# The down projection as seven products of halves, with GpSimd making the sums of its weights once

## The chip, the cores and the metric

One core of one Trainium2 chip runs the whole layer in a single launch. The metric is device microseconds (us) of one execution. The kernel before takes 3103.75 us (median of three runs, 3103.4 to 3106.19). Five engines work side by side: TensorE (PE, with its weight loads as PEld), VectorE (DVE), ScalarE (ACT), GpSimd (POOL) and SyncE (SP). They wait for one another through semaphores. DMAs are issued from SP's and POOL's queues.

## The reference, cut to what matters

Two sequences of 1024 tokens with 1024 channels go through one encoder layer. The token mixer (neighbourhood attention beside a two-way scan) is untouched. What follows it is the channel mixer, whose last product is the one that changes:

```
h = rms_norm(x, norm_ffn_pre)                                  # (tokens 1024, 1024)
gate = depthwise_conv(h @ w_gate, ffn_conv_w, ffn_conv_b)      # (1024, 2816)
f = (gelu(gate) * (h @ w_up)) @ w_down                         # w_down: (2816, 1024)
return x + rms_norm(f, norm_ffn_post)
```

All arrays are float32 in DRAM.

## The kernel before, in words

The two sequences run one after the other (`s` = 0, 1). Activations are kept with channels on the partitions, 128 at a time. Every product in float32 is made of three matmuls in a rounded format: an operand is split into a high part and the rest, and high times high, high times rest and rest times high are added up in PSUM (`product`, lines 574 to 579). Weights come in *units* of 128 x 512 (four blocks of 128 x 128): SP loads a unit into one of four `raw` slots, ACT writes its high part (`whi`, three slots, line 1130), DVE subtracts to get the rest (`wlo`, line 1636), PE uses it for 12 matmuls of 512 columns and sets `weights_used`, which frees the slot. `JOBS` lists the order of the products; `UNITS_TO` and `RELEASE` derive the units and the waits from it. SP, ACT and DVE follow this one list, each ahead of PE by as much as the slots allow.

The gate and up projections (job kind `seven`) already use seven products of halves for each of 20 of the 22 blocks of 128 of the inner width 2816: seven units a block, with DVE forming the sums of weights (lines 2098 to 2112). The result of block p is f(p), 128 x 1024 tokens, made by `f_product`. The first 12 blocks of f don't fit and are sent to DRAM by POOL (line 2482), and brought back at the end of this stage (`f_back`, lines 2486 to 2497): three transfers of 1 MB with the first halves of the tokens, then one of 3 MB with the second halves.

The down projection (job kind `down`, lines 1074 to 1092) is then 16 jobs: 2 halves of the tokens times 8 blocks of 128 output channels. A job adds up 22 blocks of f, so 22 x 3 matmuls, in one PSUM bank. f is split too: ACT writes the high part (`f_first`, line 1522), DVE the rest in place (`f_rest`, line 2125), all 22 blocks of a half at the start of that half, in the order `DOWN_CHUNKS`. After each job ACT copies the bank out (line 1569).

While the second half runs, the first four of the eight token tiles of the result are turned back by PE (`tail_tile`, line 640), normalised (`tail_stats`, `tail_out`) and saved, with `x1_ring` holding three tiles of the residual that POOL fetches (line 2324). The other four tiles come after the stage: for sequence 0 inside the start of sequence 1, for sequence 1 at the very end. In sequence 0 SP also fetches the eight tiles of the next sequence's input (`load_x`, line 526), all at once when the second half has begun, before the next weights in its queue.

## Time and profile before

| | |
|---|---|
| median of three runs | 3103.75 us |
| the profiled execution | 3104.28 us, of which the span of its records is 3102.5 us |
| granted TensorE clock, mean | 0.98 of full speed |
| PE busy | 2941.6 us (95%) |
| DVE, ACT, POOL busy | 60%, 41%, 16% |
| down projection, sequence 0 | 1282.15 to 1547.08 us |
| down projection, sequence 1 | 2821.52 to 3076.84 us |

A row of the profile names a line of the kernel, an engine, what is written and from what. PE's matmuls overlap: a row of 0.40 us stands every 0.23 us, so their pace is read from the starts. The clock is given as a share of 2.4 GHz; 0.50 would be 1.2 GHz throughout a stretch. The idle time before a row is followed by what ended it.

### The profile page before, as it was taken

Reading aid. Unit: us, or ns where it says so; the run is one execution under the profiler, and the core shown is the slowest. Engines: PE = TensorE matmul, PEld = TensorE weight load, DVE = VectorE, ACT = ScalarE, POOL = GpSimd, SP = SyncE. Lnnn points to the kernel's source line nnn. Section 1 sums busy time; section 2 is a strip of 40 time slices with the busy share of each in tenths; the row PEclk is TensorE's granted clock in tenths of the full one; section 3 lists DMA queues with packets and bytes.
Section 4 is the critical chain, followed back from the end, with each engine's and each line's share of the span. In section 5 each row is a group of like instructions: output and inputs, shape, how many; then the busy total and the mean of one; then the engine's idle time right before and its main releaser. Section 6 shows DMA issues by size and latency. Waiting matters only on the chain.

```text
span 3102.5 us, 37254 instructions
## 1 busy us (share of the span) xinstructions
PE 2941.6 (95%) x13432; PEld 2336.7 (75%) x13432; DVE 1855.1 (60%) x2915; ACT 1281.0 (41%) x2526; POOL 496.5 (16%) x730
## 2 busy tenths in 40 slices
PE   7999999899899999999999999989998999999997
PEld 5778787568678888787777787766786788887775
DVE  3657745765477777724336577457655777776342
ACT  4225555365543333424333255544655333334332
POOL 4522223540000000000000322236300000000000
PEclk9999999999999999999999999999998999999998
DMA  7441233024322211435321422331242222115342
GB/s 215 128 141 56 71 116 128 26 71 125 109 74 79 79 61 55 159 96 182 111 81 58 130 63 72 111 119 32 78 143 85 69 81 82 62 55 168 90 157 88
DMA packets 136055, 302.89 MB, mean 98 GB/s; under 512 B 16881, under 2 KB 21649, under 8 KB 135872
## 3 DMA queue, kind: packets, MB, share of 16 engines
q1 hardware_dynamic: 104848, 193.61, 20.4%
q0 software_dynamic: 31024, 106.90, 10.7%
q8 instruction: 108, 1.77, 0.2%
q14 instruction: 75, 0.61, 0.1%
HBM read 246.14 MB, written 56.26 MB: 97 GB/s over the span
## 4 chain that ended last, share of the span: by engine, by line
PE 77%; DVE 10%; issue 4%; POOL 4%; ACT 4%; DMA 1%; SPq 0%; DVEq 0%; ACTq 0%; POOLq 0%
PE G L577 11%; PE G L578 11%; PE G L579 11%; PE A L1029 4%; PE A L1028 4%; PE A L1027 4%; PE G L1027 4%; PE G L1029 4%; PE G L1028 4%; PE G L607 2%; PE G L608 2%; PE G L609 2%; PE A L748 2%; DVE arena L1783 2%; POOL arena L2411 2%
## 5 line engine op out<-in xcount | busy, mean ns | idle before, releaser
L1636 DVE TENSOR_TENSOR wlo<-raw,whi 128x512 fp32r<-128x512 f32 x620 | 418.5, 681 | 747.4 <-ACT whi L1130 746.7
L577 PE MATMUL G<-arena_rounded,whi 128*128 128x512 f32 x1792 | 730.8, 408 | 20.8 <-DVE wlo L1636 11.7
L579 PE MATMUL G<-arena_rounded,wlo 128*128 128x512 f32 x1792 | 712.0, 397 | 0.0
L578 PE MATMUL G<-arena_rounded,whi 128*128 128x512 f32 x1728 | 687.2, 398 | 0.0
L1130 ACT CAST whi<-raw 128x512 fp32r<-128x512 f32 x620 | 371.3, 608 | 571.8 <-PE G L579 451.4
L577 PEld LDWEIGHTS G<-arena_rounded,whi 128*128 128x128 f32 x1792 | 339.7, 190 | 109.2 <-issue 17.6
L579 PEld LDWEIGHTS G<-arena_rounded,wlo 128*128 128x128 f32 x1792 | 339.1, 189 | 82.1
L578 PEld LDWEIGHTS G<-arena_rounded,whi 128*128 128x128 f32 x1728 | 327.4, 189 | 76.2
L1027 PE MATMUL G<-arena_rounded,whi 128*128 128x512 f32 x560 | 221.7, 396 | 1.3 <-DVE small L2174 1.3
L1029 PE MATMUL G<-arena_rounded,wlo 128*128 128x512 f32 x560 | 221.5, 396 | 0.0
L1027 PE MATMUL A<-arena_rounded,whi 128*128 128x512 f32 x560 | 221.5, 396 | 0.0
L1028 PE MATMUL A<-arena_rounded,whi 128*128 128x512 f32 x560 | 221.5, 396 | 0.0
L1029 PE MATMUL A<-arena_rounded,wlo 128*128 128x512 f32 x560 | 221.5, 396 | 0.0
L1028 PE MATMUL G<-arena_rounded,whi 128*128 128x512 f32 x560 | 221.5, 395 | 0.0
L1130 ACT CAST whi<-small 128x512 fp32r<-128x512 f32 x160 | 99.1, 621 | 220.3 <-DVE small L2106 86.9
L607 PE MATMUL G<-whi,arena_rounded 128*128 128x512 f32 x320 | 138.5, 433 | 8.9 <-ACT small L1262 4.7
L1293 ACT ACTIVATE small<-small,nmx 128x192 f32<-128x192 f32 (+3 forms) x128 | 66.3, 518 | 188.1 <-DVE nmx L1840 188.1
L608 PE MATMUL G<-wlo,arena_rounded 128*128 128x512 f32 x320 | 126.4, 395 | 0.0
L609 PE MATMUL G<-whi,arena_rounded 128*128 128x512 f32 x320 | 126.3, 395 | 0.0
L1027 PEld LDWEIGHTS G<-arena_rounded,whi 128*128 128x128 f32 x560 | 105.2, 188 | 27.5 <-DVE small L2174 2.2
L1636 DVE TENSOR_TENSOR wlo<-small,whi 128x512 fp32r<-128x512 f32 x160 | 110.0, 687 | 24.8 <-ACT whi L1130 20.8
L1028 PEld LDWEIGHTS A<-arena_rounded,whi 128*128 128x128 f32 x560 | 105.2, 188 | 25.4
(312 smaller groups left out, 4788.2 us busy)
## 6 DMA issues: line engine op xcount, KB each, us to landing
raw<-w_gu_tiles SPq DMA_DIRECT2D x184, 256.0 KB, 3.1
raw<-w_down_tiles SPq DMA_DIRECT2D x160, 256.0 KB, 2.7
raw<-w_tok_tiles SPq DMA_DIRECT2D x96, 256.0 KB, 2.7
raw<-w_out_tiles SPq DMA_DIRECT2D x96, 256.0 KB, 2.7
raw<-w_in_tiles SPq DMA_DIRECT2D x92, 256.0 KB, 2.7
f_by_chunk<-small POOLq DMA_DIRECT2D x24, 512.0 KB, 4.5
arena<-x SPq DMA_DIRECT2D x16, 512.0 KB, 8.6
gate_by_token<-small POOLq DMA_DIRECT2D x16, 512.0 KB, 4.1
```

The lines of the kernel that those rows point to most:

```text
L577: nc.tensor.matmul(out, whi[:, u % SPLIT_SLOTS, w], hi, start=first, stop=False)
L578: nc.tensor.matmul(out, whi[:, u % SPLIT_SLOTS, w], lo, start=False, stop=False)
L579: return nc.tensor.matmul(out, wlo[:, u % SPLIT_SLOTS, w], hi, start=False, stop=last)
L607: nc.tensor.matmul(bank(i), h_hi(k, half)[:, cs], w_hi, start=k == 0, stop=False)
L608: nc.tensor.matmul(bank(i), h_hi(k, half)[:, cs], w_lo, start=False, stop=False)
L609: m = nc.tensor.matmul(bank(i), h_lo(k, half)[:, cs], w_hi, start=False, stop=k == KD - 1)
L1027: nc.tensor.matmul(bank, w_hi, hi(kk), start=kk == 0 and not onto, stop=False, skip_group_check=True)
L1028: nc.tensor.matmul(bank, w_hi, lo(kk), start=False, stop=False, skip_group_check=True)
L1029: m = nc.tensor.matmul(bank, w_lo, hi(kk), start=False, stop=kk == UC - 1, skip_group_check=True)
L1130: nc.scalar.copy(whi[:, u % SPLIT_SLOTS, w], weights_of(u)).then_inc(S["hi_split"], 1)
L1293: nc.scalar.activation(p_, p_, ACT.Exp, bias=nmx[:, st % 2:st % 2 + 1], accum_out=rsum[:, st % 2:st % 2 + 1]).then_inc(S["p_exp"], 1)
L1636: tt(wlo[:, u % SPLIT_SLOTS, w], weights_of(u), whi[:, u % SPLIT_SLOTS, w].bitcast(F), ALU.subtract).then_inc(S["lo_split"], 1)
```

## The change

The down projection is done by seven products of halves. The inner width of 2816 is cut into two sets of 11 blocks (`K1`, `K2`), the 1024 tokens and the 1024 output channels into halves of 512. Instead of eight products of half by half there are seven (`PRODUCTS`), on the halves themselves (`a11`, `a22`, `a12`) or on sums of them (`s1` to `s4`). Each runs over 11 units. A unit is now one block of 128 of the inner width by 512 output channels, for one set of four PSUM banks: 4 banks x 3 matmuls. Partial results stay in the banks from one product to the next where they are needed again (`onto`), and are copied out by ACT (`copy_down`, products 0 to 3) or added by DVE (`add_down`, products 4 to 6).

f goes through a ring of four pairs of a high part and a rest (`ring`), one pair a unit. DVE also forms the sums of f: `t1_made` in product 0, `t_made` two units ahead in products 1 to 3. The sums of the weights are made once, by GpSimd, while sequence 0 is in the gate and up stage: for each of 11 pairs of blocks two loads, four element-wise operations of 128 x 512 and two stores to DRAM (`sums_of_down`). The input of the next sequence is fetched tile by tile between weight loads (`X_LOADED`), into halves of blocks of f that are done with; the tail tiles use other banks (`tail_pair`) and stand in products 5 and 6 (`TAILS_AT`). Some semaphores for single steps of ACT are merged into one (`after`).

```diff
-JOBS += [("down", j, (h,)) for h in range(2) for j in range(KD)]
+JOBS += [("down", o, (0, 1)) for o in range(7)]
-CHUNKS = {..., "down": FK}
+CHUNKS = {..., "down": FK // 2 * UC}
...
+K1 = tuple(range(12, 20)) + (4, 5, 6)
+K2 = (7, 0, 1, 2, 3, 8, 9, 10, 11, 20, 21)
+PRODUCTS = ("a11", "s2", "s3", "a22", "a12", "s1", "s4")
+RING = (0, 1, 8, 9)
+X_LOADED = (37, 41, 57, 60, 45, 63, 66, 69)
+TAILS_AT = ((5, 3), (5, 5), (6, 0), (6, 2))
...
 # SP
-                for job in range(J_OUT + EARLY, J_DOWN + KD + 1):
+                for job in range(J_OUT + EARLY, J_DOWN + 1):
                     load(job)
-                if s + 1 < SEQS:
-                    sp.wait_ge(S["weights_used"], nth("weights_used", UNITS_TO[J_DOWN + KD]))
-                    load_x(s + 1)
-                for job in range(J_DOWN + KD + 1, len(JOBS)):
-                    load(job)
+                sp.wait_ge(S["sw_saved"], 32 * HALF_K)
+                for n in range(HALF_K, 7 * HALF_K):
+                    o, i = divmod(n, HALF_K)
+                    if n in X_LOADED and s + 1 < SEQS:
+                        at_x = X_LOADED.index(n)
+                        sp.wait_ge(S["weights_used"], nth("weights_used", UNITS_TO[J_DOWN + (3 if at_x in (0, 1, 4) else 5)]))
+                        load_x(s + 1, (at_x,))
+                    load(J_DOWN + o, slice(i, i + 1))
...
 # PE, in place of the loop over 16 jobs
+                    out, w = down_banks(o)[:, b, :], slice(b * P, (b + 1) * P)
+                    nc.tensor.matmul(out, w_hi, ring(n, 0), start=i == 0 and not onto, stop=False, skip_group_check=True)
+                    nc.tensor.matmul(out, w_hi, ring(n, 1), start=False, stop=False, skip_group_check=True)
+                    return nc.tensor.matmul(out, w_lo, ring(n, 0), start=False, stop=i == HALF_K - 1, skip_group_check=True)
...
+                for o in range(7):
+                    for i in range(HALF_K - 2):
+                        parts_ready_for(o, i)
+                        for b in range(4):
+                            if i == 0:
+                                if 1 <= o <= 3:
+                                    pe.wait_ge(S["d_copied"], nth("d_copied", 4 * (o - 1) + b + 1))
...
+                                elif o == 6:
+                                    pe.wait_ge(S["d_added"], nth("d_added", 4 + b + 1))
+                            m = part_of_down(o, i, b)
+                        m.then_inc(S["weights_used"], 1)
...
+                    for i in range(HALF_K - 2, HALF_K):
+                        parts_ready_for(o, i)
+                    for b in range(4):
+                        m = part_of_down(o, HALF_K - 2, b)
+                        if b == 3:
+                            m.then_inc(S["weights_used"], 1)
+                        m = part_of_down(o, HALF_K - 1, b)
+                        m.then_inc(S["d_done" if b < 3 else "weights_used"], 1)
...
 # ACT
+                def f_first(n):
+                    o, i = divmod(n, HALF_K)
+                    act.wait_ge(S["weights_used"], nth("weights_used", UNITS_TO[J_DOWN] + (n - 3 if n >= 4 else -6)))
...
+                    elif o < 4:
+                        act.wait_ge(S["ft_made"], nth("ft_made", n + 1))
+                    nc.scalar.copy(ring(n, 0), of_f(n)).then_inc(S["fhi_done"], 1)
...
+                for n in range(7 * HALF_K):
+                    o, i = divmod(n, HALF_K)
+                    if n >= 4:
+                        f_first(n)
+                    if i == 1 and 1 <= o <= 4:
+                        for b in range(3):
+                            copy_down(o - 1, b)
+                    split_to(UNITS_TO[J_DOWN] + n + 1)
+                    if i == 1 and 1 <= o <= 4:
+                        copy_down(o - 1, 3)
...
 # DVE
+                def t1_made(i):
+                    second_half_of(K1[i])
+                    dve.wait_ge(S["flo_done"], nth("flo_done", i + 1))
+                    tt(f_at(K1[i], 0), f_at(K1[i], 1), f_at(K1[i], 0), ALU.subtract).then_inc(S["ft_made"], 1)
...
+                    if s == 0 and p == F_KEPT + 4:
+                        dve.wait_ge(S["sw_saved"], 32 * HALF_K)
...
+                for n in range(7 * HALF_K):
+                    o, i = divmod(n, HALF_K)
+                    if n >= 4:
+                        f_rest(n)
+                    if i == 1 and o >= 5:
+                        for b in range(3):
+                            add_down(o - 1, b)
+                    split_to(UNITS_TO[J_DOWN] + n + 1)
+                    if i == 1 and o >= 5:
+                        add_down(o - 1, 3)
+                    if o == 0:
+                        t1_made(i)
+                    if HALF_K <= n + 2 < 4 * HALF_K:
+                        t_made(*divmod(n + 2, HALF_K))
...
 # POOL
+                def sums_of_down(i):
...
+                    pool.dma_start(first, w_down[K1[i]]).then_inc(S["sw_in"], 16)
+                    pool.dma_start(second, w_down[K2[i]]).then_inc(S["sw_in"], 16)
+                    pool.wait_ge(S["sw_in"], 32 * (i + 1))
+                    for to, a, b, op in ((a22, a21, a22, ALU.add), (a21, a11, a21, ALU.subtract),
+                                                        (a11, a22, a11, ALU.subtract), (a12, a12, a11, ALU.subtract)):
+                        nc.gpsimd.tensor_tensor(to, a, b, op).then_inc(S["pool_step"], 1)
+                        pool.wait_ge(S["pool_step"], step())
+                    pool.dma_start(sw_dram[i, 0], first).then_inc(S["sw_saved"], 16)
+                    pool.dma_start(sw_dram[i, 1], second).then_inc(S["sw_saved"], 16)
...
                 for p in range(F_KEPT):
                     pool.wait_ge(S["f_ready"], nth("f_ready", p + 1))
                     settled()
                     pool.dma_start(f_dram[p], f_home(p)).then_inc(S[f"f_moved{p % 2}"], 16)
+                    if s == 0 and p:
+                        sums_of_down(p - 1)
...
-                pool.wait_ge(S["weights_used"], nth("weights_used", UNITS_TO[J_DOWN + KD]))
+                pool.wait_ge(S["weights_used"], nth("weights_used", UNITS_TO[J_DOWN + 5]))
```

Three places show how the order moves. First DVE's queue from the end of the gate and up stage into the down projection. Before, `L2125` is `f_rest`, `L1636` the rest of a weight unit, `L2117` to `L2079` the last block's gate and convolution, `L2090` its product:

```order
L1636 TENSOR_TENSOR wlo<-raw,whi 128x512 x2
L2125 TENSOR_TENSOR arena_rounded<-arena,arena_rounded 128x512 x2
L2117 TENSOR_TENSOR small<-G,small 128x512
L2075 TENSOR_SCALAR small<-small,prm 128x1024
L2077 SCALAR_TENSOR_TENSOR small<-small,prm 128x1024
L2079 SCALAR_TENSOR_TENSOR small<-small,prm 128x1024
L1636 TENSOR_TENSOR wlo<-raw,whi 128x512
L2125 TENSOR_TENSOR arena_rounded<-arena,arena_rounded 128x512 x4
L1636 TENSOR_TENSOR wlo<-raw,whi 128x512
L2125 TENSOR_TENSOR arena_rounded<-arena,arena_rounded 128x512 x4
```

The same place now; `L1719` is the rest of a weight unit, `L2207` is `f_rest`, `L2224` is `t1_made`, and `L2200`, `L2158`, `L2160`, `L2162` are the gate and the convolution:

```order
L1719 TENSOR_TENSOR wlo<-raw,whi 128x512 x2
L2200 TENSOR_TENSOR small<-G,small 128x512
L2224 TENSOR_TENSOR arena<-arena 128x512 x2
L2158 TENSOR_SCALAR small<-small,prm 128x1024
L1719 TENSOR_TENSOR wlo<-raw,whi 128x512
L2224 TENSOR_TENSOR arena<-arena 128x512
L2160 SCALAR_TENSOR_TENSOR small<-small,prm 128x1024
L1719 TENSOR_TENSOR wlo<-raw,whi 128x512
L2224 TENSOR_TENSOR arena<-arena 128x512
L2162 SCALAR_TENSOR_TENSOR small<-small,prm 128x1024
L2207 TENSOR_TENSOR arena_rounded<-arena,arena_rounded 128x512
L1719 TENSOR_TENSOR wlo<-raw,whi 128x512
```

The splits of f, in fours before, stand singly beside each weight unit now, with a sum of f behind them, and the convolution is spread over three units.

Second, POOL's queue in the gate and up stage of sequence 0. Before, it has nothing there but the transfers of f to DRAM and back:

```order
L2478 MEMSET small 128x1
L2482 DMA f_by_chunk<-small 128x1024 x12
L2489 DMA arena<-f_by_chunk 128x4x512 x3
L2489 DMA arena<-f_by_chunk 128x12x512
```

Now, from the second block of f on, the sums of one pair of weight blocks follow each transfer (`L2623` are the four operations):

```order
L2633 DMA f_by_chunk<-small 128x1024 x2
L2618 DMA arena<-w_down_rows 128x1024
L2619 DMA arena<-w_down_rows 128x1024
L2623 TENSOR_TENSOR arena<-arena 128x512 x4
L2625 DMA sums_of_down<-arena 128x1024
L2626 DMA sums_of_down<-arena 128x1024
L2633 DMA f_by_chunk<-small 128x1024
```

Eleven such groups stand in the queue, and each later transfer of f is queued behind one.

Third, SP's queue in the down projection of sequence 0, where the next input is fetched. Before:

```order
L520 DMA raw<-w_down_tiles 128x512 x5
L520 DMA raw<-w_down_tiles 128x256
L526 DMA arena<-x 128x2x512 x8
L520 DMA raw<-w_down_tiles 128x512 x5
```

Now, from unit 33 on (`L567` are weights, `L573` the tiles of the input):

```order
L567 DMA raw<-w_down_rows 128x512 x4
L573 DMA arena<-x 128x2x512
L567 DMA raw<-w_down_rows 128x512 x4
L573 DMA arena<-x 128x2x512
L567 DMA raw<-w_down_rows 128x512 x4
L573 DMA arena<-x 128x2x512
L567 DMA raw<-w_down_rows 128x512 x10
L567 DMA raw<-sums_of_down 128x512 x2
L573 DMA arena<-x 128x2x512
L567 DMA raw<-sums_of_down 128x512 x3
```

Eight transfers in a row have become single ones, three before unit 46 and five from unit 57 on.

## Rows read from the trace of the kernel before

**Rows 1.** The page, part 1: busy us, share, instructions of each engine.
```profile
PE 2941.6 (95%) x13432; PEld 2336.7 (75%) x13432; DVE 1855.1 (60%) x2915; ACT 1281.0 (41%) x2526; POOL 496.5 (16%) x730
```

**Rows 2.** Stretches: length, busy us by engine, granted clock, DMA share, GB/s.
```profile
1282.15:1547.08 264.93, 255.90 (x1089) 204.24 (x1088) 102.71 (x158) 97.44 (x177) 8.63 (x12) 0.98 0.45 141
2821.52:3076.84 255.32, 251.55 (x1089) 200.93 (x1087) 97.04 (x148) 88.31 (x159) 8.24 (x12) 1.00 0.41 125
1410.00:1420.00 10.00, 10.00 (x43) 7.57 (x42) 8.12 (x14) 2.56 (x5) 0.15 (x1) 1.00 1.01 357
1430.00:1440.00 10.00, 10.00 (x32) 7.91 (x33) 5.03 (x7) 4.57 (x8) 0.68 (x1) 0.70 0.39 124
1490.00:1500.00 10.00, 10.00 (x38) 7.96 (x37) 1.71 (x3) 1.27 (x3) 0.70 (x1) 0.83 0.56 169
890.00:1260.00 370.00, 370.00 (x1587) 298.11 (x1586) 278.27 (x379) 117.44 (x191) 5.86 (x11) 1.00 0.21 70
```

**Rows 3.** Timeline of PE, last unit before the down projection: start, length, engine, line.
```profile
1276.79 0.39 PE L1028 MATMUL G<-arena_rounded,whi 128*128 128x512 f32 x1
...
1281.92 0.40 PE L1029 MATMUL G<-arena_rounded,wlo 128*128 128x512 f32 x1
```

**Rows 4.** PE groups, the first two stretches: busy, mean | idle, releasers.
```profile
L577 PE MATMUL G<-arena_rounded,whi 128*128 128x512 f32 x352 | 141.9, 403 | 9.0 <-DVE wlo L1636 5.9 <-issue 1.9 <-DVE arena_rounded L2125 1.3
...
L577 PE MATMUL G<-arena_rounded,whi 128*128 128x512 f32 x352 | 140.1, 398 | 3.8 <-issue 1.9 <-DVE arena_rounded L2125 1.3 <-DVE wlo L1636 0.6
```

**Rows 5.** Timeline of PE in sequence 0's down projection, its two longest idle times.
```profile
1429.94 0.76 PE L577 MATMUL G<-arena_rounded,whi 128*128 128x512 f32 x1 [3.67 <-DVE wlo L1636]
...
1489.45 0.50 PE L577 MATMUL G<-arena_rounded,whi 128*128 128x512 f32 x1 [2.19 <-DVE wlo L1636]
```

**Rows 6.** DMA in the stretch 1405 to 1435: KB each, median us to landing.
```profile
raw<-w_down_tiles SPq DMA_DIRECT2D x6, 256.0 KB, 9.7
```

**Rows 7.** DMA issues over the whole span, the same columns.
```profile
raw<-w_down_tiles SPq DMA_DIRECT2D x160, 256.0 KB, 2.7
...
arena<-x POOLq DMA_DIRECT2D x16, 512.0 KB, 5.6
```

**Rows 8.** Timeline of DVE after the gate and up stage of sequence 0.
```profile
1284.14 1.28 DVE L2077 SCALAR_TENSOR_TENSOR small<-small,prm 128x1024 f32<-128x1024 f32 x1
...
1290.28 2.49 DVE L2125 TENSOR_TENSOR arena_rounded<-arena,arena_rounded 128x512 fp32r<-128x512 f32 x4
...
1293.29 1.22 DVE L2090 TENSOR_TENSOR small<-small 128x1024 f32<-128x1024 f32 x1
```

**Rows 9.** Timeline of ACT there.
```profile
1290.34 2.18 ACT L1522 CAST arena_rounded<-arena 128x512 fp32r<-128x512 f32 x4
...
1299.73 0.59 ACT L1569 COPY arena<-G 128x512 f32<-128x512 f32 x1 [0.71 <-PE G L579]
```

**Rows 10.** POOL's issues of f's way back, and DMA from 1262 to 1300.
```profile
1274.22 2.52 POOL L2489 DMA_DIRECT2D arena<-f_by_chunk  x3 [5.36 <-issue]
...
arena<-f_by_chunk POOLq DMA_DIRECT2D x1, 3072.0 KB, 18.7
```

**Rows 11.** POOL's plain additions, by line: ns min/median/max, first and last start.
```profile
L2421 POOL TENSOR_TENSOR arena<-arena x14: 2364/2381/2388, 565.3 to 2193.1; 128x1024 f32<-128x1024 f32 x14
```

**Rows 12.** A GpSimd operation and the DVE operation beside it, timelines of both.
```profile
545.63 1.90 POOL L2411 TENSOR_TENSOR arena<-arena,scal 128x1024 f32<-128x1024 f32 x1 [2.17 <-PE G L773]
...
546.45 2.17 DVE L1867 TENSOR_TENSOR arena<-arena,scal 128x1024 f32<-128x1024 f32 x1
```

**Rows 13.** A weight unit in sequence 0's gate and up stage, on DVE and PE.
```profile
1035.76 0.69 DVE L1636 TENSOR_TENSOR wlo<-raw,whi 128x512 fp32r<-128x512 f32 x1 [1.63 <-ACT whi L1130]
...
1037.64 0.40 PE L1027 MATMUL G<-arena_rounded,whi 128*128 128x512 f32 x1
```

**Rows 14.** Timeline of PE where the output bank changes every three matmuls.
```profile
2033.42 0.39 PE L609 MATMUL G<-whi,arena_rounded 128*128 128x512 f32 x1
2033.65 0.40 PE L607 MATMUL G<-whi,arena_rounded 128*128 128x512 f32 x1
```

307 lines of the change are left out of this document (172 added, 135 removed).

## The prediction

> **What bounds the kernel now.** I read the busy shares first: TensorE is busy for 95% of the span, every other engine for 60% or less [rows 1]. So the question is how many matmuls the change takes away, and whether anything new makes PE wait. Next the stretches [rows 2]: the down projection takes 264.93 us in sequence 0 and 255.32 us in sequence 1. Then PE's timeline for the pace. The overlapping rows are 0.4 us long, but 22 starts lie between 1276.79 and 1281.92, so a matmul of 512 columns costs 0.2333 us [rows 3]. At full clock a unit of 12 takes 2.80 us.
>
> With that the two stretches can be split. Each holds 2 x 8 x 22 x 3 = 1056 matmuls, 246.4 us. In sequence 1 PE idled for 3.8 us [rows 4]; the other 255.32 - 246.4 - 3.8 = 5.1 us are the four tail tiles that PE turns in this stretch, and matmuls that restart after a wait. Sequence 0 idled 9.0 us [rows 4]. With the same 5.1, 264.93 - 246.4 - 9.0 - 5.1 = 4.4 us are left: after the waits of 3.67 and 2.19 us [rows 5] the granted clock is 0.70 and 0.83 in the next 10 us [rows 2], that is 6 and 3.4 us at the lower level of 1.2 GHz, which lose 3.0 and 1.7 us. The long wait is for weights: eight input tiles of 512 KB stand before them in SP's queue, and they take 9.7 us to land [rows 6] instead of 2.7 [rows 7].
>
> **What goes.** Seven products of 11 units of 12 matmuls are 924 matmuls a sequence, 215.6 us. 132 x 0.2333 = 30.8 us a sequence go whatever else happens, if the pace holds. The reason that it might not is the bank, which now changes after every three matmuls. The token-major products before do that, and the first matmul on the next bank starts 0.23 us after the last on the old one [rows 14]. I cost the change of bank at nothing.
>
> **What the other engines must do for a unit of 2.80 us.** Before, all of f is split in bursts at the start of a half, and PE waits for them (1.3 us for L2125, and 1.9 us where the second half begins [rows 4]). Now every unit needs one split of f and one of weights. ACT: 2 casts of 2.18 / 4 = 0.55 us [rows 9], 1.1 us. DVE: 2 subtractions of 2.49 / 4 = 0.62 [rows 8], plus one sum of f of the same shape in products 0 to 3, 1.9 us; in the units where both kinds of sum fall (9 and 10) 2.5 us. All are under 2.80, and slots let DVE run up to two units ahead.
>
> The start is the fullest place on DVE, so I walk through it. Before unit 8 DVE has one addition, 9 sums, 5 splits of f, 7 of weights (two were made early), a convolution of three steps of at most 1.28 and a product of 1.22 [rows 8]: 22 x 0.62 + 5.1 = 18.7 us from the end of the old stage at 1282.3, so about 1301. PE wants unit 8 at 1282.15 + 8 x 2.80 = 1304.6. That eighth sum also needs f's second halves back from DRAM. They were not needed before the second half of the stage; now they are needed at about 1300. POOL issues the last transfer at about 1276 and it lands 18.7 us later [rows 10], 1294.7. Margin 5 us; cost nothing. Behind this sum on DVE stands the split for unit 9, which PE wants at 1307.4; if f came later than about 1305, PE would wait for it.
>
> At the end of a product the last two units run bank by bank, so bank 0 is complete 18 matmuls, 4.2 us, before bank 3. ACT's copy of 0.59 us [rows 9] of bank 3 starts about 0.2 after the product's end; the next product reaches bank 3 after nine matmuls, 2.1 us. Slack 1.3 us. Between products 5 and 6 DVE adds instead, with a weight split ahead of the last addition: slack about 0.6 us. Cost nothing, up to the 1.9 us of a job change before [rows 4] for each of the 12 changes.
>
> So sequence 1: 215.6 + 5.1 = 220.7 us, 34.6 saved (30.8 of matmuls, 3.8 of waits).
>
> **The new wait of sequence 0.** SP may fetch the third input tile only when product 4 has ended, and unit 57 stands behind that tile in its queue; behind unit 57 wait the further weights, and for these ACT, DVE and PE. PE arrives at unit 57 two units, 5.6 us, after that moment. At the same moment POOL fetches three tiles of 512 KB. A busy stretch moved 357 GB/s [rows 2]. If SP's 0.79 MB share this evenly with POOL, they need 4.4 us, with 2.0 for the landing (2.7 less the 0.7 of 256 KB at that rate), 0.65 for the issues and 1.3 for cast and subtraction: 8.3 us, a wait of 2.7. Had SP all the rate, 0.6; were POOL served first, 5.0. I take 2.5 and 1.4 for the clock afterwards, near the 1.7 that followed the wait of 2.19. The earlier tiles (units 37, 41, 45) wait for the end of product 2, but unit 37 is cast four units after it, so they hide. Sequence 0: 220.7 + 3.9 = 224.6, 40.3 saved.
>
> **GpSimd's sums.** They run in the gate and up stage of sequence 0, whose PE has no idle time: 370 of 370 us busy [rows 2]. One block takes 84 x 0.2333 = 19.6 us. One group of sums is two loads (5.6 us [rows 7], about 7 for both), four additions of 2.38 / 2 = 1.19 us [rows 11], and issues and semaphores: about 14 us. So POOL keeps up, and its transfer of the next block of f isn't late. The 23 MB moved add some 100 GB/s to 70, against 357 that were reached.
>
> But the additions touch DVE. Beside a GpSimd operation that ran from 545.63 to 547.53 a DVE operation with two inputs in SBUF took 2.17 us, and it ended 1.1 us after GpSimd's [rows 12]; one of the same size takes 1.22 [rows 8]. It had waited for the other to end. The Trainium skill states this as a rule against the change ("SBUF — State Buffer", "Who interferes with whom"): of GpSimd and such a DVE operation, whichever issues second blocks until the first ends. The trace agrees. Four additions can then hold DVE for up to 4 x 1.19 = 4.8 us a block. DVE is 75% busy there (278 of 370 [rows 2]), so 4.9 us of idle time a block can take it up, but in small pieces, one of 1.63 [rows 13]. The subtraction behind that one ends at 1036.45, and PE starts its unit at 1037.64 [rows 13]: a delay over 1.2 us there reaches PE. A group starts about 7 us after the block's f, in the looser part. Bounds: nothing, and 11 blocks x (4.8 - 1.2) = 40 us. I take 0.3 a block, 3 us.
>
> **The rest.** The end: DVE's addition of 0.69 takes the place of ACT's copy of 0.59, and the chain behind it (turn, normalise, fetch the last residual tile, save) stays: nothing. The passage from sequence 0 to 1 keeps its order: nothing, or 2 us less.
>
> **Sum.** Against the profiled execution: 3104.28 - 34.6 - 40.3 + 3 = 3032.4. The median of the runs is 0.5 lower: 3032.
>
> **Rivals.**
>
> *A. DVE is held by GpSimd at the wrong place.* For it: the row of 2.17 us, and the slack of only 1.2. Against it: the alignment above, and that it strikes only one sequence. At 1.5 us a block 16 instead of 3: 3045; at the bound 3069.
>
> *B. Product changes cost.* For it: 12 changes at which ACT or DVE must clear four banks in step with PE, with slacks of 0.6 to 1.3 us. Against it: bank 0 is ready 4.2 us early. At 1.5 us each, 18 us: 3050.
>
> *C. The clock falls, and the change loses.* Units wait a little each, for a split or a bank, and the stretch runs at a granted clock of 0.70, as 1430 to 1440 did [rows 2]: 431.2 us of matmuls become 616, 185 more: 3217. It decides from a mean of 431 / (431 + 72) = 0.86 downwards in the two stretches. For it: two waits did lower the clock. Against it: in sequence 1 waits of 1.9 us and less left it at 1.00 over the whole stretch [rows 2, 4], and in the new stage I find one wait above that. The Trainium skill describes such a case ("TensorE: Matmul & The Clock Gate", "A second HAM failure mode: psum-queue depth-cycling"): products that cycle through banks leave PE short pauses, and its clock swings between the levels. By that rule this rival would be likely; [rows 14] show bank changes without a pause.
>
> That the change doesn't do what it says is excluded for PE: its queue holds 264 matmuls of 512 columns fewer.
>
> **How the numbers follow.** Forecast 0.70, A 0.13, B 0.10, C or something else as dear 0.05, a gain eaten up to nothing 0.02. The lower end: sequence 0 without its new waits (-3.9), GpSimd free (-3), the passage 2 shorter and about 2 of restarts gone: 3021. The upper end holds the dear bound of unit 57 (5.0 + 3.0 for the clock, +4) with either B (+18) or 2 us a block of A (+19) and some of the other: 3060. About 0.2%, 6 us, is what a measurement of this kernel can tell from no change. Faster 0.93 (forecast, A, B), same 0.02, slower 0.05.
>
> **What would show it.** Right: 0.2333 us between starts inside products; in sequence 1's down projection near 221 us with hardly any idle time at lines 1133 to 1135; in sequence 0's one wait of 1 to 5 us at the third unit of product 5; unchanged pace at the gate and up stage, with DVE's subtractions longer where GpSimd adds. Wrong: idle time at each product's first unit (B), at every block of sequence 0's gate and up stage (A), or a granted clock below 0.9 in the down projections (C); and a wait at unit 8 or 9, if f's second halves come late.

## The result, and the profile after

The changed kernel takes 3033.16 us (median of four runs, 3029.28 to 3035.28) against 3103.57 for the kernel before beside it: a ratio of 0.977, interval 0.9755 to 0.9784. The forecast was 3032, with a range of 3021 to 3060. The profiled execution is the fastest of the four, 3029.28 us, of which its records span 3027.5.

Busy time by engine, the row that answers to [rows 1]:

```profile
PE 2875.5 (95%) x13168; PEld 2285.6 (75%) x13168; DVE 1970.3 (65%) x3055; ACT 1301.6 (43%) x2554; POOL 599.0 (20%) x818
```

PE issues 13168 instead of 13432 matmuls. For that DVE is busy for 115 us more than before, ACT for 21 and POOL for 102.5. The stretches of the changed kernel, columns as in [rows 2]: gate and up of sequence 0, its down projection, and that of sequence 1.

```profile
868.59:1288.41 419.82, 416.51 (x1776) 332.73 (x1777) 337.05 (x421) 137.14 (x219) 110.44 (x104) 1.00 0.38 130
1288.41:1509.86 221.45, 219.74 (x957) 176.92 (x956) 149.47 (x230) 110.51 (x196) 8.28 (x12) 1.00 0.47 155
2782.54:3001.82 219.28, 219.28 (x957) 176.83 (x955) 143.88 (x220) 101.23 (x178) 8.26 (x12) 1.00 0.41 134
```

The down projections fell by 43.5 and 36.0 us, and the granted clock is 1.00 in both. The gate and up stage of sequence 0, which the change doesn't touch on PE, took 415.39 us before and now takes 419.82. In the other 2141.2 us (ahead of that stage, and between the two down projections) nothing is gained or lost in these two profiles: 866.76 + 1274.44 before, 868.59 + 1272.68 after. Over all profiles of this document, before and after the change, the same stretches take 2137.3 to 2143.0 us, though the experiments change nothing of PE's work there: a time moves by some us for reasons that lie outside the stages compared here. The end tail is 25.7 in both.

The first matmul of a bank's three carries a product's waits. PE's groups of that line in the two down projections answer to [rows 4] (busy and mean, then the idle time and who ended it): 1.7 us of idle time in sequence 0, none in sequence 1.

```profile
L1133 PE MATMUL A<-arena_rounded,whi 128*128 128x512 f32 x264 | 105.1, 398 | 1.7 <-DVE wlo L1719 1.7
...
L1133 PE MATMUL A<-arena_rounded,whi 128*128 128x512 f32 x264 | 104.9, 398 | 0.0
```

PE's timeline of sequence 0's down projection has two idle times left where before it had several, [rows 5] among them:

```profile
1449.67 0.50 PE L1133 MATMUL A<-arena_rounded,whi 128*128 128x512 f32 x1 [1.50 <-DVE wlo L1719]
...
1471.65 0.47 PE L1133 MATMUL A<-arena_rounded,whi 128*128 128x512 f32 x1 [0.21 <-DVE wlo L1719]
```

The first is unit 57, the place that the prediction named. SP's queue shows the wait as it was described: the input tile's issue, and with it the three weight loads behind it, come 12.57 us after the load before.

```profile
1430.04 0.33 SPq L567 DMA_DIRECT2D raw<-sums_of_down  x1
1442.61 0.55 SPq L573 DMA_DIRECT2D arena<-x  x1
1443.20 1.62 SPq L567 DMA_DIRECT2D raw<-sums_of_down  x3
```

New is idle time of PE in the gate and up stage, 3.25 us at four places (before: one of 0.65 near the end of the stage):

```profile
922.64 0.47 PE L1080 MATMUL G<-arena_rounded,whi 128*128 128x512 f32 x1 [0.54 <-DVE wlo L1719]
...
1061.42 0.47 PE L1080 MATMUL A<-arena_rounded,whi 128*128 128x512 f32 x1 [0.77 <-DVE wlo L1719]
...
1079.50 0.50 PE L1080 MATMUL G<-arena_rounded,whi 128*128 128x512 f32 x1 [0.97 <-DVE small L2287]
...
1083.53 0.47 PE L1080 MATMUL G<-arena_rounded,whi 128*128 128x512 f32 x1 [0.97 <-DVE wlo L1719]
```

The releaser is DVE each time. Its groups from 890 to 1275 show why. Some of the operations with all their inputs in SBUF are longer than in the same stage without GpSimd's additions (the rows of that run follow under *no_adds*): the splits and the convolution's step are, the first sums of weights in the last row aren't.

```profile
L1719 DVE TENSOR_TENSOR wlo<-small,whi 128x512 fp32r<-128x512 f32 x78 | 63.3, 812 | 9.5 <-ACT whi L1218 7.5
L1719 DVE TENSOR_TENSOR wlo<-raw,whi 128x512 fp32r<-128x512 f32 x57 | 43.1, 756 | 40.4 <-ACT whi L1218 39.6
L2160 DVE SCALAR_TENSOR_TENSOR small<-small,prm 128x1024 f32<-128x1024 f32 x19 | 30.1, 1585 | 0.7
...
L2187 DVE TENSOR_TENSOR small<-raw 128x512 f32<-128x512 f32 x19 | 13.1, 689 | 10.0 <-DMA raw<-w_gu_tiles 10.0
```

Two causes could stand behind that: GpSimd's additions hold DVE (theory 1), or the 23 MB of the sums' transfers make the stage's own weights late (theory 2; for it speaks the last row, 10.0 us of waiting for raw weights).

### The profile page after: what moved, and what is told of

It reads as the page before. It is cut to its first block, busy times and chain, and to the rows that moved or that the text cites. A ratio compares the mean times of both kernels' runs of the same rounds, so it can differ in the third digit from the quotient of the medians.

```text
span 3027.5 us, 37119 instructions
## 1 busy us (share of the span) xinstructions
PE 2875.5 (95%) x13168; PEld 2285.6 (75%) x13168; DVE 1970.3 (65%) x3055; ACT 1301.6 (43%) x2554; POOL 599.0 (20%) x818
## 3 DMA queue, kind: packets, MB, share of 16 engines
q8 instruction: 107, 1.75, 0.2%
## 4 chain that ended last, share of the span: by engine, by line
PE 77%; DVE 10%; issue 5%; POOL 4%; ACT 4%; DMA 1%; SPq 0%; DVEq 0%; ACTq 0%; POOLq 0%
PE G L627 7%; PE G L628 7%; PE G L629 7%; PE A L1080 4%; PE A L1082 4%; PE A L1081 4%; PE A L1133 4%; PE A L1135 4%; PE A L1134 4%; PE G L1080 4%; PE G L1082 4%; PE G L1081 4%; PE G L657 2%; PE G L658 2%; PE G L659 2%
## 5 line engine op out<-in xcount | busy, mean ns | idle before, releaser
L1719 DVE TENSOR_TENSOR wlo<-raw,whi 128x512 fp32r<-128x512 f32 x582 | 406.0, 702 | 566.0 <-ACT whi L1218 564.3
L1218 ACT CAST whi<-raw 128x512 fp32r<-128x512 f32 x582 | 355.3, 620 | 477.1 <-PE G L629 173.3
L627 PE MATMUL G<-arena_rounded,whi 128*128 128x512 f32 x1088 | 449.2, 413 | 8.5 <-DVE wlo L1719 5.8
L628 PE MATMUL G<-arena_rounded,whi 128*128 128x512 f32 x1088 | 432.8, 398 | 0.0
L629 PE MATMUL G<-arena_rounded,wlo 128*128 128x512 f32 x1088 | 432.4, 397 | 0.0
L627 PEld LDWEIGHTS G<-arena_rounded,whi 128*128 128x128 f32 x1088 | 206.5, 190 | 59.4 <-issue 4.2
L629 PEld LDWEIGHTS G<-arena_rounded,wlo 128*128 128x128 f32 x1088 | 206.0, 189 | 49.6
L628 PEld LDWEIGHTS G<-arena_rounded,whi 128*128 128x128 f32 x1088 | 206.4, 190 | 47.5
L1080 PE MATMUL G<-arena_rounded,whi 128*128 128x512 f32 x560 | 222.6, 397 | 2.6 <-DVE wlo L1719 1.5
L1080 PE MATMUL A<-arena_rounded,whi 128*128 128x512 f32 x560 | 222.0, 396 | 0.8 <-DVE wlo L1719 0.8
L1082 PE MATMUL A<-arena_rounded,wlo 128*128 128x512 f32 x560 | 221.7, 396 | 0.0
L1082 PE MATMUL G<-arena_rounded,wlo 128*128 128x512 f32 x560 | 221.7, 396 | 0.0
L1081 PE MATMUL G<-arena_rounded,whi 128*128 128x512 f32 x560 | 221.7, 396 | 0.0
L1081 PE MATMUL A<-arena_rounded,whi 128*128 128x512 f32 x560 | 221.6, 396 | 0.0
L1133 PE MATMUL A<-arena_rounded,whi 128*128 128x512 f32 x528 | 210.1, 398 | 1.7 <-DVE wlo L1719 1.7
L1134 PE MATMUL A<-arena_rounded,whi 128*128 128x512 f32 x528 | 209.0, 396 | 0.0
L1135 PE MATMUL A<-arena_rounded,wlo 128*128 128x512 f32 x528 | 209.0, 396 | 0.0
L657 PE MATMUL G<-whi,arena_rounded 128*128 128x512 f32 x320 | 138.6, 433 | 8.9 <-ACT small L1348 4.7
L1719 DVE TENSOR_TENSOR wlo<-small,whi 128x512 fp32r<-128x512 f32 x160 | 119.7, 748 | 22.1 <-ACT whi L1218 18.1
L1080 PEld LDWEIGHTS G<-arena_rounded,whi 128*128 128x128 f32 x560 | 105.3, 188 | 31.3 <-issue 2.7
```

Of the source, the lines that this page charges most:

```text
L627: nc.tensor.matmul(out, whi[:, u % SPLIT_SLOTS, w], hi, start=first, stop=False)
L628: nc.tensor.matmul(out, whi[:, u % SPLIT_SLOTS, w], lo, start=False, stop=False)
L629: return nc.tensor.matmul(out, wlo[:, u % SPLIT_SLOTS, w], hi, start=False, stop=last)
L657: nc.tensor.matmul(bank(i), h_hi(k, half)[:, cs], w_hi, start=k == 0, stop=False)
L1080: nc.tensor.matmul(bank, w_hi, hi(kk), start=kk == 0 and not onto, stop=False, skip_group_check=True)
L1081: nc.tensor.matmul(bank, w_hi, lo(kk), start=False, stop=False, skip_group_check=True)
```

## The experiments

All ran beside the kernel before (3103.87 to 3105.8 us in these comparisons). *Lost by PE* is, in the gate and up stage of sequence 0, the sum over all matmuls of how much later than 0.2333 us after its predecessor one starts, where that is over 0.04 us (good to 0.1 us); the kernel before has 1.01, and its stage takes 415.39. The *gate/up* and *down* columns come from the one profiled execution of each kernel, the medians from all of its runs.

| kernel | median, us | ratio, interval | gate/up s0 | lost by PE there | down s0 | down s1 |
|---|---|---|---|---|---|---|
| changed | 3033.16 | 0.9755-0.9784 | 419.82 | 5.51 | 221.45 | 219.28 |
| no_adds | 3021.41 | 0.9719-0.9746 | 414.78 | 0.40 | 221.24 | 219.25 |
| no_moves | 3025.93 | 0.9734-0.9761 | 417.10 | 2.87 | 220.86 | 219.23 |
| no_sums | 3023.49 | 0.9726-0.9753 | 414.79 | 0.39 | 220.54 | 219.28 |
| x_later | 3026.18 | 0.9735-0.9762 | 421.26 | 6.96 | 219.54 | 219.25 |
| early4 | 3033.66 | 0.9759-0.979 | 426.44 | 12.14 | 219.51 | 219.24 |
| early22 | 3023.57 | 0.9725-0.9754 | 416.44 | 2.01 | 219.52 | 219.25 |
| more_matmuls | 3090.3 | 0.9934-0.9966 | 418.44 | 4.03 | 251.99 | 250.04 |
| ring1 | 3572.15 | 1.149-1.1526 | 419.11 | 4.69 | 494.0 | 489.6 |
| ring2 | 3103.76 | 0.9987-1.0006 | 417.56 | 3.16 | 259.85 | 256.12 |
| plain_end | 3027.49 | 0.9734-0.9763 | 418.45 | 4.13 | 221.33 | 219.09 |
| side_a (changed again) | 3031.26 | 0.9744-0.977 | 417.78 | 3.39 | 220.77 | 219.25 |
| side_b (early22 again) | 3022.88 | 0.9723-0.975 | 414.81 | 0.31 | 219.52 | 219.27 |

### no_adds, no_moves, no_sums: what costs time in the gate and up stage

```diff
 # no_adds: loads and stores stay
-                    for to, a, b, op in ((a22, a21, a22, ALU.add), ...):
-                        nc.gpsimd.tensor_tensor(to, a, b, op).then_inc(S["pool_step"], 1)
 # no_moves: the operations stay
-                    pool.dma_start(first, w_down[K1[i]]).then_inc(S["sw_in"], 16)
-                    pool.dma_start(second, w_down[K2[i]]).then_inc(S["sw_in"], 16)
-                    pool.dma_start(sw_dram[i, 0], first).then_inc(S["sw_saved"], 16)
-                    pool.dma_start(sw_dram[i, 1], second).then_inc(S["sw_saved"], 16)
 # no_sums (in this and in no_moves the waits for the sums go too)
-                        sums_of_down(p - 1)
```

> The changed kernel without GpSimd's four element-wise operations a group: the loads and stores of the sums stay, so the weights of the sums are stored unsummed (that part of the computation is left out). Theory 1 (the additions hold DVE's operations with two inputs in SBUF): the gate and up stage of sequence 0 falls from 419.8 us back to 415 to 416.5, its DVE operations return to 0.69 us for a split, the four waits of PE before that line's splits (3.25 us in sum) go, and the kernel takes about 4 us less, 3029. Theory 2 (the sums' transfers make the stage's raw weights late): the stage stays at 419 to 420, DVE still waits some 10 us for raw weights before the first sum of a block, and the kernel stays at 3033. If both act, the stage lands between, near 418.

> The changed kernel with GpSimd's four element-wise operations a group, 11 groups, but without the two loads and two stores of each (they work on whatever lies there, and the down projection reads unsummed weights in place of the sums, from another array of the same size: that part of the computation is left out). Theory 1 (the additions hold DVE): the gate and up stage of sequence 0 stays at 418.5 to 420 us, with DVE's splits at about 0.8 to 0.9 us on average, and the kernel at about 3033. Theory 2 (transfers): it falls to 415 to 416.5, and the wait for raw weights before a block's first sum falls from about 10 us in sum to the 3 us of before; kernel about 3029.

> The changed kernel without GpSimd's sums altogether, neither operations nor transfers; the down projection reads unsummed weights in place of the sums (that part of the computation is left out). Both theories: the gate and up stage of sequence 0 takes 415.4 us as before the change (415 to 416), kernel about 3029. If it stays near 419, the loss there comes neither from the additions nor from their transfers but from the changed order elsewhere. The down projections keep 221.5 and 219.3 us.

Without the additions the stage takes 414.78 us, as without any sums (414.79), and PE loses 0.40 us, although all 23 MB still move (131 GB/s in the stage, 130 in the changed kernel). Both kernels came out faster than expected, 3021.41 and 3023.49 us instead of 3029: their medians fell by 10 to 12 us where the stage gives 5. In the profile of *no_adds* 2.7 us more lie in the stretches that no experiment changes, so the argument goes by the stages. DVE's groups of *no_adds* in the same stretch:

```profile
L1719 DVE TENSOR_TENSOR wlo<-small,whi 128x512 fp32r<-128x512 f32 x78 | 53.6, 688 | 12.7 <-ACT whi L1218 10.6
L1719 DVE TENSOR_TENSOR wlo<-raw,whi 128x512 fp32r<-128x512 f32 x58 | 40.0, 690 | 51.8 <-ACT whi L1218 51.8
L2160 DVE SCALAR_TENSOR_TENSOR small<-small,prm 128x1024 f32<-128x1024 f32 x19 | 24.4, 1286 | 0.7
...
L2187 DVE TENSOR_TENSOR small<-raw 128x512 f32<-128x512 f32 x19 | 13.1, 690 | 2.7 <-DMA raw<-w_gu_tiles 2.6
```

The wait for raw weights went from 10.0 to 2.7 us with the transfers in place, so theory 2 falls. A load also lands as soon: 3.3 us after its issue in both kernels, 3.2 before the change. SP may load a unit only when an older one is split, so late splits make late loads. Theory 1 says that the additions hold DVE, and they do it without transfers too, with splits of 0.76 and 0.89 us on average, as it said. But in two points *no_moves* did not behave as theory 1 expected: the stage took 417.1 us, not 418.5 to 420, and other operations were lengthened. Its DVE groups of the same stretch:

```profile
L1718 DVE TENSOR_TENSOR wlo<-raw,whi 128x512 fp32r<-128x512 f32 x57 | 50.9, 892 | 38.6 <-ACT whi L1217 38.6
L2186 DVE TENSOR_TENSOR small<-raw 128x512 f32<-128x512 f32 x19 | 25.1, 1319 | 0.2 <-DMA raw<-w_gu_tiles 0.2
L2159 DVE SCALAR_TENSOR_TENSOR small<-small,prm 128x1024 f32<-128x1024 f32 x19 | 24.4, 1285 | 0.7
```

Here the first sums of the next block were nearly doubled (1319 ns) and the convolution untouched (1285). Without loads to wait for, the four additions started 0.6 us after the save of f instead of 8 to 10, and PE lost a steady 0.3 us a block. So the transfers may matter after all, by *when* they let the additions start.

### x_later: the wait at unit 57

```diff
-X_LOADED = (37, 41, 57, 60, 45, 63, 66, 69)
+X_LOADED = (37, 41, 59, 61, 45, 63, 66, 69)
```

> The changed kernel with the third and fourth input tile fetched before units 59 and 61 instead of 57 and 60. Theory (PE's 1.5 us at unit 57 is the wait of SP's queue for the end of product 4, behind which that unit's load stands): the wait at unit 57 goes, the down projection of sequence 0 falls from 221.45 to about 219.8 us, near sequence 1's 219.33, and the kernel takes 1.5 us less. Rival (the tiles themselves are too much for the queue, wherever they stand): a wait of 1 us or more turns up at units 60 to 63 instead, and the stage stays at 221 to 222.

The wait is gone, none took its place, and the stage takes 219.54 us, 0.3 from sequence 1's. The median fell by 7 us instead of 1.5, although the gate and up stage took 1.4 us longer in the profile: the two medians come from different sets of runs, and only the stage can be read here.

### early4 and early22: does the place of the additions decide?

```diff
                     pool.wait_ge(S["sw_in"], 32 * (i + 1))
+                    if i + 1 < HALF_K:
+                        loads_of_down(i + 1)
                     for to, a, b, op in (...):
+                        if to is a11:      # early22 alone
+                            pool.wait_ge(S["weights_used"], nth("weights_used", UNITS_TO[j_seven(i + 3)] + 2))
                         nc.gpsimd.tensor_tensor(to, a, b, op).then_inc(S["pool_step"], 1)
```

> The changed kernel with the input tiles moved as in x_later, and with the loads of each group of sums issued one block of f ahead, so that the four additions start about 2 us after the save of f instead of 8 to 10 (where the kernel with additions and no transfers had them: PE lost 2.87 us there, 0.3 a block, against 5.51 in the changed kernel and 6.96 in x_later). Theory (where in a block the additions hold DVE decides, the transfers cost nothing): the gate and up stage of sequence 0 takes 417 to 418 us, 2 to 4 less than x_later's 421.3, the kernel some 3 us less than x_later's 3026, 3023. Rival (additions beside transfers cost what they cost, wherever they stand): the stage stays at 420 to 421, the kernel at 3026.

> As early4, but only two of the four additions start right after the save of f, the other two when PE has done two units of the next block, some 10 us later. Theory (DVE has some 3 us to spare at either place, and PE loses only what a longer hold takes beyond that): PE loses under 1 us, the stage takes 414.8 to 415.8 us, as without the additions, and the kernel about 3020 to 3021. Rival (each single addition of 1.6 to 1.75 us is longer than the slack, so that their number decides): the stage takes 417 us or more, as in early4.

*early4* became the worst of all, 426.44 us: nine blocks in a row lose 0.9 to 1.3 us each at one place, a wait for DVE's split. That is neither theory's number. The additions start 1.6 us after POOL begins to issue the save of f, behind the issues of the next loads, instead of 0.6 in *no_moves*, and PE loses four times as much, though the same DVE operations are held for about as long (splits of `raw` 892 ns in both, first sums 1318 and 1319). *early22* took the loss away but for one block, which lost 1.2 us. Its stage, 416.44 us, lies between theory and rival, and its kernel, 3023.57, is 3 us above the theory; its second run, *side_b*, came to the theory's stage (414.81). POOL's timeline of it shows the two pairs in a block of 19.6 us, 3.02 and 3.54 us long:

```profile
942.17 0.53 POOL L2641 DMA_DIRECT2D f_by_chunk<-small  x1 [2.07 <-DVE small L2173]
943.92 0.54 POOL L2616 DMA_DIRECT2D arena<-w_down_rows  x1 [1.22 <-DMA sums_of_down<-arena]
944.45 0.54 POOL L2617 DMA_DIRECT2D arena<-w_down_rows  x1
945.00 3.02 POOL L2630 TENSOR_TENSOR arena<-arena 128x512 f32<-128x512 f32 x2
954.46 3.54 POOL L2630 TENSOR_TENSOR arena<-arena 128x512 f32<-128x512 f32 x2 [6.44 <-PE G L1082]
```

### side_a and side_b: both once more, side by side

> The changed kernel once more, on the same chip and in the same rounds as early22 once more (side_b). Its runs so far ranged from 3029 to 3035 us, while kernels that differ from it by a wait of 1.5 us gave 3025 to 3030. Theory (that the additions fall where they fall, and PE loses 4 to 7 us by them from run to run): 3029 to 3035 again, 6 to 10 us above side_b. Rival (the chip or the hour made the difference): 3025 to 3028, 2 to 5 us above side_b.

> early22 once more, beside the changed kernel itself: two additions right after the save of f, two some 10 us later, loads one block ahead, input tiles three and four fetched before units 59 and 61. By the stages read so far (down projection of sequence 0 219.5 against 221.5, gate and up stage 416.4 against 419.8) it should be 5.4 us faster than side_a, 3021 to 3026 us. If the two lie within 2 us, the stages gained there are lost elsewhere.

Side by side the changed kernel takes 3031.26 us (3027.97 to 3031.94) and *early22* 3022.88 (3020.98 to 3026.85): 8.4 us less, without overlap, as the theory of *side_a* expected (6 to 10). *early22* beats both the kernel before and the changed one. Its gate and up stage and down projection of sequence 0, as *side_b* has them:

```profile
866.27:1281.08 414.81, 414.77 (x1777) 333.43 (x1777) 337.11 (x421) 136.36 (x219) 103.67 (x102) 1.00 0.37 129
1281.08:1500.60 219.52, 219.31 (x957) 176.76 (x956) 149.38 (x230) 110.56 (x196) 8.28 (x12) 1.00 0.47 156
```

DVE is busy for 337.11 us, as long as in the changed kernel (337.05) and 24 us longer than in *no_adds* (313.39). DVE is held just as long, and PE loses 0.31 us instead of 5.51, no more than without additions. What differs is the place, and that the four additions stand in two pairs; no run separates the two. That the place counts by itself shows between *early4* and *x_later*: four additions in a row in both, the loads and additions at other times, 12.14 and 6.96 us. The changed kernel's own loss is not constant: it was 5.51 us in one profile and 3.39 in the other, and the stage took 417.6 to 421.3 us in the seven profiles in which the additions start when their loads land. These two stretches explain 4.2 of the 5.5 us between the two profiled executions. Why the medians lie 8.4 apart isn't settled: only the profiled runs can be looked into.

### more_matmuls: is the gain the count?

```diff
-                        for b in range(4):
+                        for b in range(4) if o != 1 else (0, 1, 2, 3, 0, 1, 2, 3):
...
+                        if o == 1:
+                            part_of_down(o, HALF_K - 2, b)
+                            part_of_down(o, HALF_K - 2, b)
```

> The changed kernel with every matmul of product 1 issued twice, 132 more matmuls of 512 columns in each sequence, as many as the change takes away (that product counts double in the result, so the computation is another one). Theory (the number of matmuls at 0.2333 us makes the gain): 30.8 us a sequence come back, the down projections take 252 and 250 us, and the kernel 3033 + 61.6 = 3095 us; that is less than the kernel before by the waits and the clock lost in its down projections, 18 us, less what the gate and up stage lost. Rival (the gain came from the order: waits, banks, the clock): the kernel gains back less than 45 us, as the doubled product leaves the other engines more time, and lands below 3078.

Doubling a product gave back 30.5 and 30.8 us in the two stretches, 57 to 59 us in the medians (61.6 expected). The count explains the matmuls' share to 0.3 us a sequence; the rest of the gain is the waits and the clock that went with the old stage.

### ring1 and ring2: what would have made the change lose?

```diff
-RING = (0, 1, 8, 9)
+RING = (0,)          # ring1 (with the end of a product in plain order); ring2: (0, 8)
...
-    ... UNITS_TO[J_DOWN] + (n - 3 if n >= 4 else -6)
+    ... UNITS_TO[J_DOWN] + (n if n >= 1 else -6)          # ring2: n - 1 if n >= 2
```

Fewer parts of f are made ahead to match, and in *ring1* the copies and additions of banks come one unit earlier.

> The changed kernel with one pair instead of four in the ring of f's parts, and the last two units of a product in plain order: every unit must wait until the unit before it is done, then for a cast of 0.55 and a subtraction of 0.62 us, so PE pauses some 1.5 to 2 us after every 2.80 us of work. Theory 1 (short pauses don't lower the granted clock, as in the down projections of the two kernels): clock 1.00 in both stretches, each 110 to 155 us longer, kernel 3250 to 3345. Theory 2 (my rival C: regular short pauses lower it to 0.70 or so): the pace inside a unit falls to 0.467 us for part of the time, and the matmuls alone cost 185 us more on top: 3435 to 3530.

> The changed kernel with two pairs instead of four in the ring of f's parts. In ring1 PE waited 2.04 us after every unit of a sequence (the chain: cast of f, cast of weights, rest of f, rest of weights, 2.4 to 2.7 us from a unit's end), and its pace fell to 0.43 us a matmul within a few of them, granted clock 0.78. With two pairs that chain starts one unit of 2.80 us earlier, so it just fits; only at a product's first unit, where the unit before the last ends 0.7 us before the last, PE waits about 2 us, six times a sequence. Theory 1 (seldom pauses leave the clock at 1.00): each down projection 10 to 20 us longer, kernel 3053 to 3073. Theory 2 (pauses of 2 us lower it for the following 10 us, as the waits of 2.2 and 3.7 us did before the change): granted clock 0.85 to 0.95, each stretch 30 us or more longer, kernel above 3090.

*ring1* lost more than either theory said, and rival C's mechanism is real, though waits make up more of the loss than the clock. The two down projections of *ring1*:

```profile
1285.88:1779.90 494.02, 333.92 (x957) 238.29 (x956) 151.94 (x233) 110.17 (x199) 8.27 (x12) 0.78 0.21 70
3055.60:3545.20 489.60, 329.69 (x957) 234.54 (x955) 146.79 (x223) 101.17 (x181) 8.27 (x12) 0.78 0.18 60
```

The granted clock is 0.78. PE's timeline within a unit there, starts 0.23 us apart at first and 0.43 after the fifth matmul:

```profile
1348.65 0.50 PE L1133 MATMUL A<-arena_rounded,whi 128*128 128x512 f32 x1 [2.04 <-DVE wlo L1717]
1348.98 0.39 PE L1134 MATMUL A<-arena_rounded,whi 128*128 128x512 f32 x1
...
1349.91 0.58 PE L1135 MATMUL A<-arena_rounded,wlo 128*128 128x512 f32 x1
1350.30 0.63 PE L1133 MATMUL A<-arena_rounded,whi 128*128 128x512 f32 x1
1350.72 0.63 PE L1134 MATMUL A<-arena_rounded,whi 128*128 128x512 f32 x1
```

From the starts of sequence 0: the waits cost 172 us (72 of them, 2.4 us each from start to start beyond the pace), and 436 matmuls at 0.43 us instead of 0.2333, with the steps between, cost 98. Theory 1 was wrong on the clock and theory 2 on the waits, which I had put at 110 to 155 us.

*ring2* takes the kernel back to 3103.76 us, the time of before, with 264 matmuls fewer. The expectation had six pauses a sequence; there are 15 rows with idle time. PE's timeline of sequence 0 has, for product 0, both kinds:

```profile
1314.47 0.47 PE L1133 MATMUL A<-arena_rounded,whi 128*128 128x512 f32 x1 [2.24 <-DVE wlo L1718]
...
1315.56 0.63 PE L1133 MATMUL A<-arena_rounded,whi 128*128 128x512 f32 x1
...
1323.48 0.47 PE L1133 MATMUL A<-arena_rounded,whi 128*128 128x512 f32 x1 [1.62 <-ACT arena L1615]
```

One stands at unit 9, which I had not counted: bank by bank, units 9 and 10 are both needed before either begins, and unit 10's pair is free only after unit 8. The other stands at the next product's start. In sequence 0 the waits cost 31.4 us and the lower clock 9.7, from the starts: after three of the five waits of 2.24 us, and after those of 3.52 and 3.84, seven or eight matmuls ran at 0.43 us, after none of those of 1.34 to 1.62. In sequence 1 the clock fell after a wait of 2.63 us and not after one of 2.79, so the length of the wait alone did not decide. The granted clock is 0.97 in both stretches, between the two theories. So the stretch's 38 us are mostly waits: the time came out where theory 2 had it, but mostly by waits at more places than either had counted.

### plain_end: the changes of product

```diff
                     for i in range(HALF_K - 2, HALF_K):
                         parts_ready_for(o, i)
-                    for b in range(4):
-                        m = part_of_down(o, HALF_K - 2, b)
...
+                        for b in range(4):
+                            m = part_of_down(o, i, b)
```

> The changed kernel with the last two units of a product in plain order, unit by unit, so that bank 0 is complete 2.1 instead of 4.2 us before bank 3. My sum priced the changes of product at nothing, by slacks of 0.6 to 1.3 us at bank 3, which this doesn't change; at bank 0 a copy of 0.59 us and its semaphores then have 2.1 us before the product's end. Theory (slack is left at each change): no waits at the first units of a product, the down projections stay at 221.5 and 219.3 us, the kernel at 3033. Rival B (a change is tight, and the order by banks hides it): waits of 0.5 us or more at the 12 changes, 6 us or more in sum, kernel 3040 or more.

221.33 and 219.09 us, no idle time at any product's start, so the slack is real. The kernel, 3027.49 us, is below the 3033 expected, with stages that account for 1.7 us of it. With four pairs in the ring the order by banks isn't needed. (Unit 57 waited 1.97 us in this run, and the granted clock stayed at 1.00.)

## Why the prediction was right, step by step

**The count and the pace.** Right. The banks change every three matmuls without a gap. PE's timeline from the second bank of the stage to the third, answering to [rows 14]:

```profile
1289.58 0.40 PE L1135 MATMUL A<-arena_rounded,wlo 128*128 128x512 f32 x1
1289.81 0.40 PE L1133 MATMUL A<-arena_rounded,whi 128*128 128x512 f32 x1
```

0.23 us. *more_matmuls* confirms 0.2333 us a matmul in place.

**Sequence 1, 220.7 forecast, 219.28 measured.** 215.6 of it are the matmuls, so what I carried over for tail tiles and restarts, 5.1 us, is 3.7 now. How much of the 1.4 us went with the restarts wasn't separated.

**Sequence 0, 224.6 forecast, 221.45 measured.** Mechanism right, size too dear. The wait at unit 57 is 1.50 us here (0.7 to 1.97 over the profiles that have it), not 2.5, and the 1.4 us for the clock behind it were not lost: 1.00. In *plain_end* a wait of 1.97 us here left the clock alone as well, and in *ring2* 2.24 lowered it in some cases: my price had taken the wait of 2.19 of before [rows 5] as the model for a shorter one.

**f's second halves from DRAM, cost nothing.** Right, margin 4 instead of 5 us. The transfer is issued at about 1282.2 and takes 20.5 us instead of 18.7 [rows 10], so it lands at about 1302.7; the ninth sum of f that needs it starts at 1306.73, and no idle time of DVE is ended by it.

**GpSimd's sums, 3 us forecast, 4.4 measured (rival A's mechanism).** The direction and order of size were right, and the place, at splits for the next unit. That the 3 us are so near is partly luck: in the seven profiles of this stage with the additions as they are here it took 2.2 to 5.9 us more than before, and the loss stands at a few blocks, not 0.3 in each. The group starts 8 to 10 us after the block's f, not 7, and that part was not as loose as I took it.

The estimate of 1.19 us for an addition, half of a row of twice the columns [rows 11], held for the addition itself. POOL's group of the changed kernel has 1.75:

```profile
L2623 POOL TENSOR_TENSOR arena<-arena 128x512 f32<-128x512 f32 x44 | 77.0, 1749 | 85.8 <-DMA arena<-w_down_rows 83.2
```

But the single additions range from 1.28 to 2.36 us, and the difference is GpSimd waiting for DVE, which the prediction left out. Three additions of one group, and DVE beside them:

```profile
936.49 1.64 POOL L2623 TENSOR_TENSOR arena<-arena 128x512 f32<-128x512 f32 x1
938.20 2.16 POOL L2623 TENSOR_TENSOR arena<-arena 128x512 f32<-128x512 f32 x1
940.45 1.29 POOL L2623 TENSOR_TENSOR arena<-arena 128x512 f32<-128x512 f32 x1
...
937.00 0.69 DVE L2287 TENSOR_TENSOR small<-A,small 128x512 f32<-128x512 f32 x1
937.61 1.60 DVE L2162 SCALAR_TENSOR_TENSOR small<-small,prm 128x1024 f32<-128x1024 f32 x1
940.84 1.45 DVE L1719 TENSOR_TENSOR wlo<-raw,whi 128x512 fp32r<-128x512 f32 x1 [1.63 <-ACT whi L1218]
```

The addition at 940.45 finds DVE idle and takes 1.29 us. The one at 938.20 begins while a convolution's step still has 1.01 us to go, and takes 2.16: that rest and 1.15. So it is for 35 of the 44, which last 1.13 to 1.17 us beyond the end of the DVE operation in progress. DVE's split at 940.84 in turn ends 0.55 us after the addition, 1.45 us long instead of 0.69. L2287, which reads `A` in PSUM, keeps its 0.69 beside an addition. The Trainium skill ("SBUF — State Buffer", "Who interferes with whom") has DVE operations with two SBUF inputs contend with a GpSimd instruction that reads SBUF. The trace agrees: the convolution's step went from 1286 to 1585 ns on average in the changed kernel, with GpSimd's additions beside it. What this costs the kernel is another matter: with the same 44 additions PE lost between 0.3 and 12 us, without them 0.4.

**Rival B, product changes.** Nothing at any of the 12, by the changed kernel's trace and by *plain_end*.

**Rival C, the clock.** It did not come here, and with fewer pairs in the ring it does. The Trainium skill ("TensorE: Matmul & The Clock Gate", "A second HAM failure mode: psum-queue depth-cycling") has a kernel that cycles through banks leave PE short idles, and these swing the clock. In the changed kernel the banks cycle and leave no idle time, and the clock stays at 1.00; in *ring1* a pause of 2.04 us before most units goes with a granted 0.78. My chance of 0.05 rested on the reading that the new stage would have but one wait above 1.9 us; in the changed kernel it has none, the longest is 1.50.

**The sum.** Against the profiled executions: -36.0, -43.5, +4.4, and nothing elsewhere give 3029.2, where the profiled execution took 3029.28; the forecast was 3032.4, so three terms missed by -1.4, -3.2 and +1.4 us. That the median, 3033.16, lies within 1.2 us of the 3032 forecast is partly luck: the profiled execution was the fastest of its four.

## What to carry to other kernels

When a change takes matmuls away, the gain is their count times the pace only as long as the operands arrive in time: with two pairs instead of four in one ring the kernel took 3103.76 us, as before the change. Work handed to an idle engine isn't free if it shares something with a loaded one. What it costs depends on where in the loop it falls and in what portions: with the same 44 additions PE lost between 0.3 and 12 us, so pin them to places with slack by a wait instead of letting a transfer's landing choose. The loss of a resource that is busy for 95% of the time needs to be read from starts, not from idle rows alone: of the 2.87 us that PE lost in *no_moves*, idle rows show 0.4.

## What the runs showed of the hardware

- GpSimd and DVE on SBUF: a subtraction of 690 ns averages 812, a first sum 1319 instead of 690, a convolution's step 1585 instead of 1286, each depending on which of them the additions met. GpSimd waits too: an addition of 128x512 took 1.28 to 1.30 us where it didn't wait for DVE, and otherwise the rest of DVE's operation and 1.13 to 1.17 us. In sum, beside *no_adds* DVE was busy for 24 us more in the changed kernel and in *side_b*, and for 46 more in *early4* (359.71 against 313.39).
- The clock: a steady rhythm of 2.04 us of waiting and 12 matmuls runs at a granted 0.78, with about half of the matmuls at 0.43 us; in *ring2* single waits of 2.24 us cost seven or eight slow matmuls in some cases and none in others, one of 2.79 none; waits of 1.97 us and less cost none in the down projections of the changed kernel, *ring2* and *plain_end*.
